# A two-layer decoder trunk: layer 0's first norm moved behind the projections

## The reference, cut to what matters

```python
def rms_norm(x, g):
    y = x * lax.rsqrt(jnp.mean(x * x, axis=-1, keepdims=True) + EPS)
    return y * g
# layer 0, mixers (x: 256 tokens x 1024)
z = rms_norm(h, e_norm_mix[j]) @ e_w_in[j]
b_gate, c_gate, u, q, k, v = jnp.split(z, splits_even, axis=-1)
a_out = short_conv_mixer(b_gate, c_gate, u, e_conv_w[j])  # b * causal_conv3(c * u)
b_out = sliding_window_attention(q, k, v, e_sinks[j], rel_bias)  # 8 heads, 2 kv heads
h = h + jnp.concatenate([a_out, b_out], axis=-1) @ e_w_out[j]
...
# then: dense SwiGLU, per-layer embedding; layer 1: attention, top-2-of-8 experts, embedding
```

## Time and profile before

| | us |
|---|---|
| median of 3 runs | 1446.2 (1445.81 to 1446.91) |
| the profiled execution, its own time | 1446.03 |
| its span (first to last instruction) | 1444.3 |
| PE busy | 1424.7 (99%) |
| DVE busy | 1148.1 (79%) |
| ACT busy | 965.1 (67%) |
| DMA, share of 16 engines | 81.1% SP's queue, 3.3% POOL's, 1.1% ACT's |

### The profile page before, as it was taken

One profiled execution on the slowest core, in us unless ns is written; L12 is line 12 of the kernel. 1 busy time (PEld: TensorE's weight loads), 2 busy tenths in 40 slices (PEclk: granted clock), 3 DMA queues, 4 the chain that ended last, 5 costly groups with the idle time before them and its releaser, 6 DMA issues.

```text
span 1444.3 us, 19890 instructions
## 1 busy us (share of the span) xinstructions
PE 1424.7 (99%) x7083; PEld 1197.8 (83%) x7083; DVE 1148.1 (79%) x981; ACT 965.1 (67%) x890; POOL 88.4 (6%) x96
## 2 busy tenths in 40 slices
PE   9999999999999999999999999999999999999997
PEld 8978888889997888888888888888888888888885
DVE  5766444467666988988988988988898898898996
ACT  5445443455546777777777877777777787777774
POOL 2000000000002860000000000000000000002000
PEclk9999999999999999999999999999999999999999
DMA  9647755564543999999999999999999999999990
GB/s 324 225 143 281 255 199 177 201 230 152 174 146 113 388 399 395 395 393 379 378 396 378 362 395 388 354 397 392 373 378 392 378 366 394 381 343 397 396 353 30
DMA packets 197798, 454.59 MB, mean 315 GB/s; under 512 B 7481, under 2 KB 28997, under 8 KB 197758
## 3 DMA queue, kind: packets, MB, share of 16 engines
q1 hardware_dynamic: 190944, 429.94, 81.1%
q0 software_dynamic: 5040, 17.92, 3.3%
q10 hardware_dynamic: 1774, 6.17, 1.1%
HBM read 439.30 MB, written 14.70 MB: 314 GB/s over the span
## 4 chain that ended last, share of the span: by engine, by line
PE 90%; DVE 5%; ACT 3%; DMA 1%; issue 1%; ACTq 0%; SPq 0%; DVEq 0%
PE bank L1467 21%; PE bank L942 15%; PE bank L1448 14%; PE bank L1452 14%; PE bank L1455 14%; PE bank L1241 4%; PE bank L976 3%; DVE w_lo L1541 2%; PE bank L1434 2%; ACT w_hi L562 1%; DMA raw<-in_o_exp_down 1%; PE bank L1137 1%; PE bank L1042 1%; PE bank L1415 0%; ACT xn L578 0%
## 5 line engine op out<-in xcount | busy, mean ns | idle before, releaser
L1541 DVE TENSOR_TENSOR w_lo<-raw,w_hi 128x2048 fp32r<-128x2048 f32 x406 | 926.9, 2292 | 223.6 <-ACT w_hi L562 222.4
L562 ACT ACTIVATE w_hi<-raw 128x2048 fp32r<-128x2048 f32 x406 | 779.6, 1920 | 342.2 <-PE bank L1455 144.2
L1448 PE MATMUL bank<-w_hi,x_hi 128*128 128x512 f32 x896 | 244.8, 395 | 0.0
L1452 PE MATMUL bank<-w_hi,x_lo 128*128 128x512 f32 x896 | 240.1, 390 | 0.0
L1455 PE MATMUL bank<-w_lo,x_hi 128*128 128x512 f32 x896 | 239.7, 389 | 0.0
L1452 PEld LDWEIGHTS bank<-w_hi,x_lo 128*128 128x128 f32 x896 | 168.3, 188 | 35.9
L1455 PEld LDWEIGHTS bank<-w_lo,x_hi 128*128 128x128 f32 x896 | 168.2, 188 | 35.2 <-DVE w_lo L1541 0.2
L1448 PEld LDWEIGHTS bank<-w_hi,x_hi 128*128 128x128 f32 x896 | 164.2, 188 | 30.6
L1467 PE MATMUL bank<-w_hi,m_lo 128*128 128x512 f32 x448 | 121.3, 390 | 0.1
L1467 PE MATMUL bank<-w_lo,m_hi 128*128 128x512 f32 x448 | 121.1, 389 | 0.0
L1467 PE MATMUL bank<-w_hi,m_hi 128*128 128x512 f32 x448 | 120.7, 391 | 0.0
(11 more groups left out here) (266 smaller groups left out, 1335.1 us busy)
## 6 DMA issues: line engine op xcount, KB each, us to landing
raw<-in_o_exp_gate SPq DMA_DIRECT2D x112, 1024.0 KB, 6.9
raw<-in_o_exp_up SPq DMA_DIRECT2D x112, 1024.0 KB, 7.6
raw<-in_o_exp_down SPq DMA_DIRECT2D x112, 1024.0 KB, 7.5
raw<-in_o_w_qkv SPq DMA_DIRECT2D x12, 1024.0 KB, 5.1
raw<-in_e_ffn_gate SPq DMA_DIRECT2D x11, 1024.0 KB, 5.2
raw<-in_e_ffn_up SPq DMA_DIRECT2D x11, 1024.0 KB, 5.2
raw<-in_e_ffn_down SPq DMA_DIRECT2D x11, 1024.0 KB, 5.2
raw<-in_e_w_in SPq DMA_DIRECT2D x9, 1024.0 KB, 15.5
```

The lines of the kernel that those rows point to most:

```text
L562: act.activation(w_hi[:, slot % SPLIT], raw[:, slot], ACT.Copy).then_inc(hi_made, 1)
L1448: pe.matmul(dst, x_hi[:, c + kk, 0:P], hi[:, kk], start=(c, kk) == (0, 0), stop=False)
L1452: pe.matmul(dst, x_lo[:, c + kk, 0:P], hi[:, kk], start=False, stop=False)
L1541: ve.tensor_tensor(w_lo[:, slot % SPLIT], raw[:, slot], w_hi[:, slot % SPLIT], ALU.subtract).then_inc(lo_made, 1)
```

## The change

1. **Turned raw.** PE turns x itself (`turn_input`) when each half has landed; ACT and DVE read it with the gain. x is squared later, behind the first splits. The root goes in behind: by `q_scale` in `maxima` (q), by `rrow`, a row of roots that PE spreads over the partitions, into `k0T`, by `rrow2` (its square, for c times u) into c and by `rrow` into `conv_y`, by ACT's scale into v.
2. **First weights.** The first q tile comes in four loads of 256 KB, and ACT and DVE split it chunk by chunk. The products of chunk k stand together, and the diagonals' two products stand behind chunks 0 and 1. DVE copies the diagonals now.
3. **Constants.** ACT loads the identity alone at first, and the rest (`cst`) between its splits. Gains come as rows of 128, layer 0's first gain by itself.
4. **Values turned.** v is projected by feature like k (24 products of 256 columns for 48 of 128), copied, turned back (2), and scaled in four copies.
5. **Splits follow small steps.** In layer 0's attention DVE's `beside(hd)` goes behind `maxima(hd + 2)`, and ACT's split behind the copy of the probabilities. `out_tile(0)` waits for `conv_lo_made` 1 and `conv_made` 2; `out_tile(1)` for `conv_lo_made` 2.

```diff
@@ SP
-            for i in range(2):
-                load(Q0_T + i, cols_of(w_in, 3 * SC, HALF, 4 * i, 4))
+            for k in range(4):
+                sp.dma_start(raw[:, Q0_T, k * HALF:(k + 1) * HALF], w_in[k * P:(k + 1) * P, 3 * SC:3 * SC + HALF])\
+                  .then_inc(q_loaded[k] if k < 3 else tile_loaded[Q0_T], 16)
+            load(Q0_T + 1, cols_of(w_in, 3 * SC, HALF, 4, 4))
@@ ACT, norm 0
+                    act.wait_ge(gainT_made, 1)
+                    for k in range(4):
+                        act.wait_ge(xT_ready, k // 2 + 1)
+                        act.activation(x_hi[:, k, :], ..., ACT.Copy, scale=gainT[:, 0, k:k + 1]).then_inc(x_hi_made, 1)
+                        act.wait_ge(q_loaded[k] if k < 3 else tile_loaded[Q0_T], 16)
+                        act.activation(chunk_by_group(w_hi[:, Q0_T], k, True), ...)
+                    highs(i, 1)
+                    act.dma_start(cst[:, P:], consts[:, P:]).then_inc(cst_loaded, 16)
+                    between()
                     for q in range(4):
                         square(i, q)
-                    for l in range(2):
-                        act.wait_ge(diag_ready, l + 1)
-                        act.activation(diag[...], bank[2 + l][...], ACT.Copy).then_inc(diag_copied, 1)
@@ PE
+            for part, (v, x) in enumerate(((0, x_hi), (1, x_hi), (0, x_lo))):
+                for k in range(4):
+                    ...
+                    for j in range(4):
+                        mm = pe.matmul(q_out(j), w[v][:, k, j * P:(j + 1) * P], x[:, k], ...)
+                    if part == 0 and k < 2:
+                        diagonals(k)
...
+            row_of_rstd(1, 2)
             pe.wait_ge(q0_made, 4)
             pe.wait_ge(aux_loaded, 80)
+            pe.wait_ge(gain_rows_loaded, 16 * 5)
+            pe.transpose(bank[1][:, 64:64 + 5 * KC], gain_rows, ...)
@@ DVE
+            split_chunk(0)
+            split_chunk(1)
+            copy_diagonals(0)
+            split_chunk(2)
+            copy_diagonals(1)
+            split_chunk(3)
...
+            rsqrt(0)
+            rstd_diag()
...
@@ DVE, attention
-                    extra(hd)
...
                     if hd + 2 < HEADS and (layer == 0 or hd % 2):
                         maxima(hd + 2)
+                    if layer == 0:
+                        extra(hd)
@@ PE, out_tile
-                if i == 0:
-                    pe.wait_ge(conv_lo_made, 2)
+                if i < 2:
+                    pe.wait_ge(conv_lo_made, i + 1)
+                if i == 0:
+                    pe.wait_ge(conv_made, 2)
```

265 lines of the change are left out of this document (163 added, 102 removed).

## The result

The changed kernel takes **1448.5 us** (median of 12 runs, 1447.62 to 1450.6), the kernel before 1445.6 (12 runs beside it): a ratio of 1.0021 [1.0013, 1.0029], **2.9 us slower where 5.9 were forecast**. The direction was right, and the forecast twice as large as the measured change. The profiled execution of after is 1447.62, the lowest of the 12.

The account below looks back on a forecast made before the run. PE, 90% of the chain of work, was taken as the bound. Later conv_tile(0) +3.4, half rate behind the idle piece +1.9 and attention +0.6 gave +5.9 us, a median of 1452.1, range 1444.5 to 1455.0.

Parts of the forecast that it names:

- the front: Up to conv_tile(0): it starts 3.4 us later because of late loads, plus 1.9 of half rate after PE's idleness.
- the waits removed: First attention: PE's two waits on DVE's m_lo, both behind a split, go, for -1.2 us.
- the third place: Ahead of out_tile(0): PE's wait for DVE's bank-freeing multiplication grows from 1.7 to 3.5 us, for +1.8.
- the attention's gain: First attention: moving splits behind small steps saves only PE's two m_lo waits, -1.2 us.
- POOL's loads: Front: diagonals copied 5.8 us later, so r_raw lands at 38.0 instead of 32.2; PE stands from 33.0.
- The half rate behind it: Behind PE's 5 us idle piece before conv_tile(0): lost clock costs 1.9 us; out_tile(0)'s half rate stays before and after.
- Half rate at the start: PE in chunks 0 and 1 and the diagonals, 11 to 16 us: half rate, a chunk's four products taking 1.0.
- Table load exposed: ACT at the start: table load stands behind the wait for turned x, from about 8.9, exposing 1.28 us.
- k and v in 5.8: Projections of k and v: 48 products of 256 columns take 5.8 us, not 8.19; turned values win 2.4.
- Diagonals earlier: Front rival, chance 0.26: full rate or hidden table load; with both, copied at 12.7, conv_tile(0) at 35.8, 1448.5 us.
- Faster: Front rival, chance 0.14: loads land before PE arrives at 33.0; 1440.4 to 1442.2, or 1443.6 to 1445.2 us.
- Worse: Rival, chance 0.10: longer half rate after idleness or at out_tile(0), or ACT's table-load drain; 1454 to 1457 us.

Follow-up runs that it names:

- e8: Kernel before with the changed order of the small steps and the wide output products in the first attention, old front; 1442.1 us, ratio 0.9974.
- e18: e8 plus the late root's added VectorE steps (scores scaled in two parts, conv_y and c multiplied by ones); 1444.1 us, ratio 0.9989.
- e10: Kernel before with only v laid out twice and first-attention output products 128 columns of weights wide; 1445.4 us, ratio 0.9996.
- e7: Kernel before with only the changed order of the small steps and out_tile's waits in the first attention, products 64 wide; 1444.0 us, ratio 0.9988.
- e4: Changed kernel with the first attention's output products 64 columns of weights wide, as before, instead of 128; 1451.8 us, ratio 1.0045.
- e13: Changed kernel's front with the first attention as before: old order of the small steps, 64 columns of weights; 1452.9 us, ratio 1.0046.
- e1: Changed kernel with POOL's loads of sinks, taps, p and r_raw issued before its wait for the copied diagonals; 1446.1 us, ratio 0.9999.
- e5: Changed kernel with both diagonals' products in PE's idle piece ahead of chunk 0, DVE's copies directly behind their chunk's split; 1446.5 us, ratio 1.0004.
- e2: Changed kernel with ACT copying one element of zeros ahead of its first data wait, so its table load runs early; 1446.3 us, ratio 1.0005.
- e3: Changed kernel with DVE's bank-freeing multiplication of the second conv_y moved ahead of the fifth head's probabilities and maxima; 1444.5 us, ratio 0.9990.
- e17: Kernel before with all the late root's added VectorE steps in the first attention, values multiplied by one; 1447.2 us, ratio 1.0012.
- e15: Kernel before with VectorE scaling the first attention's scores in two instructions (128 and 256 wide) instead of one; 1445.7 us, ratio 1.0004.

## Why the prediction was right in direction and wrong in size

The measured sum, each term from a pair of medians: order and width together, e8 less before, **-3.5**; the root's steps in the attention, e18 less e8, **+2.0**; all else of the front, after less e18, **+4.4**. In all +2.9; each term is known to some 1 to 2 us. The prediction's terms: the waits removed -1.2, the third place +1.8, the front +5.3, in all +5.9. The two lists do not cut alike: some 0.7 of the third place's idle piece is in the -3.5 (1.69 before, 2.36 in e8). The profile of after gives the same in the prediction's own cut: the attention is 1.9 shorter although its idle piece grew by 1.8, so all else in it won 3.7 where 1.2 was forecast. Two terms were off.

- **The step that failed is the attention's gain: -1.2 forecast, -3.5 measured (-3.7 in the profile, the idle piece left aside).** It priced the moved splits by the one wait that they removed, and the wider output products at nothing. The wait was only the part by which the round through both splits was longer than PE's own head: when PE's head got shorter alone, the waits grew from 1.2 to 2.1 (e10). With the order changed PE sets the pace, and then its 0.29 a head count. The order alone fits the prediction's price (e7); what it had at nothing is the width behind it. Read in a window, the chain of before has no PE in it from 42.0 to 82.7; the prediction read it over the whole span, where PE is 90%.
- **The front was mis-sized by 0.9 (5.3 for 4.4),** which is within what the medians tell, and within the spread of the front itself: e4 and e13, at half rate from chunk 0 on as the prediction took it, have their first scores 5.5 and 5.1 later than before. In the profile of after, `conv_tile(0)` starts at 39.70 where 39.4 was worked out, and the loads land at 37.0 for 38.0: the diagonals were copied at 15.93 (16.3), `bias` issued at 21.70 (22), landing 10.9 after the issue (11.6). The mechanism of POOL's loads is right (e1, e5). The two parts inside were wrong against each other: PE was there at 34.50 and not at 30 to 33, since the q tiles ended at 28.31, later than before and not between no earlier and 3 us earlier, so it stood 2.5 and not 5.0. The half rate behind it cost 0.8 in the turns of p (1.86 for 1.03) and 0.55 in the tile (6.31 for 5.76), 1.4 for the 1.9 taken. That the start of the tile came so near to 39.4 is partly luck: the landing was 1.0 early, and the way from it to the tile took 2.7 and not 1.4.
- **Half rate at the start** was taken and is what came, but at another place: chunks 0 and 1 were faster than taken (0.71 and 0.80), but the q tile's remaining 40 products took 7.21 instead of 4.99 (e2). It was put down to chunks 0 and 1 and the diagonals only, and it was this that ate PE's lead.
- **Table load exposed, 1.28:** at 9.28, not 8.9. The Trainium skill, "ScalarE: Activation LUTs", section "What ACT_TABLE_LOAD costs", puts a drain of about 1.38 on top. The trace does not agree: x_hi starts at 10.58, 0.02 behind the load's end. An estimate from that page's figure would put the copied diagonals near 17.3; they were copied at 15.93.
- **Third place, idle 3.5:** 3.46, and from the cause that was counted (e18). The half rate behind it is there before and after, as said: 7.30 both times. (It is not always as long: 8.05 in e18 behind the same 3.46.)
- **k and v in 5.8:** 5.76. The wait of PE's output products for `m_lo` is gone, as said.
- **Rivals.** "Diagonals earlier" gave 1448.5, the measured time, but by a way that did not happen: the diagonals came at 15.93, not at 12.7, and `conv_tile(0)` started at 39.70, not at 35.8. That the time is this rival's is chance. "Faster" needed the loads by 33.0, and they landed at 37.0; e1 shows that it takes another issue order, and then `conv_tile(0)` starts at 37.70, not at 31.4. (Its time for a landing at 33.0 should read 1443.4 and not 1443.6: 33.0 + 1.4 is 1.6 ahead of 35.99, and 1.2 more goes.) "Worse" did not come.

## What to carry to other kernels

Read the chain of waits in a window of the stage that is changed, not over the whole span: a stage can go round through other engines while PE is 90% of the whole, and a wait of 1.2 us on the busy engine then hides a second bound just above its own. Two edits can be worth 1.5 and 0.3 alone there and 3.6 together, so try them together before one is thrown out. When work is moved ahead of others on one engine, look at what the queue behind it issues: the same front that lost 4.4 us lost none of it (1437.3 with the moved multiplication, where the old front with it has 1438.8) once five loads that depend on nothing stood ahead of the queue's wait, and one table load ahead of ACT's.

## What the runs showed of the hardware

- A short idle piece of PE costs more than itself. 1.3 us ahead of the q projection became 4.3 at its end (after against e2), 2.7 ahead of `out_tile(0)` became 4.3 (e3).
- At the start the record of the clock does not always show the rate. In e4_narrow the stretch below reads 1.00, yet the four products of chunk 0 (11.72 to 12.92) took 1.20, which is half rate; in after the record also reads 1.00 from 11.7 to 12.4, and they took 0.71. The same front ended its q tiles at 29.73 and at 28.31.

```profile
12.00:16.00 4.00, 4.00 (x12) 1.75 (x11) 2.14 (x4) 4.00 (x10) 0.00 (x0) 1.00 1.09 356
```

- Going from weights 128 columns wide to 64 and back cost PE 0.14 and 0.15 us (e4_narrow's chain against after's). Here it was cheaper to compute an output twice.
- A scoring instruction of VectorE with its factor in memory took 0.34 and 0.47 (128 and 256 wide; after, e17), with an immediate 0.28 and 0.41 (e15).
